# Four edits around the mixture-of-experts stages of a two-block float32 network: score banks by head, up rows beside the ring, last tile's logits token-major, a gathering quarter inside the first gate

## The reference

```python
aff = softmax(h @ router)                       # 16 experts
gate, idx = top_k(swapaxes(aff, 1, 2), cap)     # every expert takes 32 tokens of each stream
xs = h[bidx, idx]
hid = silu(einsum('becd,edf->becf', xs, w_gate)) * einsum('becd,edf->becf', xs, w_up)
y = einsum('becf,efd->becd', hid, w_down) * gate[..., None]
return zeros_like(h).at[bidx, idx].add(y)
```

## Time and profile before

| | us |
|---|---|
| median of 3 runs (2447.03 to 2451.07) | 2450.55 |
| profiled execution, its own time | 2450.56 |
| its span, first to last instruction | 2448.4 |
| TensorE busy | 2302.1 |
| VectorE busy | 1230.4 |
| ScalarE busy | 402.9 |
| DMA: 658.43 MB, mean rate over the span | 269 GB/s |
| mean granted clock of TensorE | 0.994 |

### The profile page before, as it was taken

One profiled execution on the slowest core, in us unless ns is written; L12 is line 12 of the kernel. 1 busy time (PEld: TensorE's weight loads), 2 busy tenths in 40 slices (PEclk: granted clock), 3 DMA queues, 4 the chain that ended last, 5 costly groups with the idle time before them and its releaser, 6 DMA issues. The chain is left out here.

```text
span 2448.4 us, 31994 instructions
## 1 busy us (share of the span) xinstructions
PE 2302.1 (94%) x13618; PEld 1477.8 (60%) x13618; DVE 1230.4 (50%) x2141; ACT 402.9 (16%) x885; POOL 38.6 (2%) x69
## 2 busy tenths in 40 slices
PE   8999999999999999999999998898899999988887
PEld 8898799499987994746644433333488543222222
DVE  7987777689877876935633221212265631111111
ACT  1221100002211010215621100000232420000001
POOL 0000000000000010000000000000000000000000
PEclk9999999999999999999999999999999999999999
DMA  9655765476557664512228999999941299999997
GB/s 325 241 166 197 229 211 213 158 258 241 172 190 247 201 227 143 212 45 52 93 110 349 421 429 427 427 427 428 404 150 35 94 359 416 428 427 428 428 428 321
DMA packets 170128, 658.43 MB, mean 269 GB/s; under 512 B 8551, under 2 KB 56163, under 8 KB 145411
## 3 DMA queue, kind: packets, MB, share of 16 engines
q1 hardware_dynamic: 164304, 639.66, 67.0%
q0 software_dynamic: 5312, 16.57, 2.2%
q10 hardware_dynamic: 370, 0.15, 0.0%
HBM read 655.12 MB, written 1.23 MB: 268 GB/s over the span
## 5 line engine op out<-in xcount | busy, mean ns | idle before, releaser
L881 PE MATMUL psum<-ring,arena 128*64 128x512 f32 (+2 forms) x2036 | 437.6, 583 | 56.1 <-DMA ring<-in_moe_w_up 35.3
L881 PEld LDWEIGHTS psum<-ring,arena 128*64 128x64 f32 (+1 forms) x2036 | 128.3, 123 | 338.8 <-issue 301.1
L912 PE MATMUL psum<-ring,lnp 128*32 128x512 f32 (+1 forms) x988 | 223.4, 598 | 35.2 <-DMA ring<-in_moe_w_down 34.9
L1806 DVE TENSOR_TENSOR lnp<-arena,psum 128x512 f32<-128x512 f32 (+2 forms) x32 | 33.8, 1056 | 411.5 <-PE psum L881 403.4
L1816 DVE TENSOR_TENSOR arena<-psum,spare 32x512 f32<-32x512 f32 x96 | 65.8, 686 | 230.3 <-PE psum L912 229.4
L2496 PE MATMUL psum<-ht,ring 128*128 128x128 f32 x1472 | 174.7, 277 | 2.5 <-DMA ring<-in_w_in 2.5
L912 PEld LDWEIGHTS psum<-ring,lnp 128*32 128x32 f32 (+1 forms) x988 | 63.7, 123 | 187.4 <-issue 149.7
L2496 PEld LDWEIGHTS psum<-ht,ring 128*128 128x128 f32 x1472 | 169.6, 193 | 6.3 <-issue 6.3
L580 PE MATMUL psum<-ring,ht 128*128 128x512 f32 x320 | 140.0, 594 | 0.0
L1227 ACT ACTIVATE lnp<-psum 128x512 f32<-128x512 f32 (+1 forms) x32 | 15.7, 490 | 625.6 <-PE psum L842 620.0
L2930 DVE SCALAR_TENSOR_TENSOR spare<-ring,arena,spare 128x512 f32<-128x512 f32 x168 | 113.8, 745 | 0.0
(11 more groups left out here) (555 smaller groups left out, 3278.1 us busy)
## 6 DMA issues: line engine op xcount, KB each, us to landing
ring<-in_moe_w_gate SPq DMA_DIRECT2D x62, 2048.0 KB
ring<-in_moe_w_up SPq DMA_DIRECT2D x61, 2048.0 KB
ring<-in_moe_w_down SPq DMA_DIRECT2D x57, 2048.0 KB
ring<-in_w_in SPq DMA_DIRECT2D x51, 1024.0 KB, 9.0
ring<-in_ada_w SPq DMA_DIRECT2D x48, 1024.0 KB
ring<-in_w_ffn_gate SPq DMA_DIRECT2D x22, 1024.0 KB
ring<-in_w_ffn_up SPq DMA_DIRECT2D x22, 1024.0 KB
ring<-in_w_ffn_down SPq DMA_DIRECT2D x20, 1024.0 KB
```

The lines of the kernel that those rows point to most:

```text
L881: last = mm(bank[w * j:w * j + w, 0:cols], (x_last if layer else x_four)[:, k, e % 4, :], row[:, cols * j:cols * j + cols], start=k == 0, ...
L912: last = mm(bank[w * j:w * j + w, :], hidT[:, e % 2, a:a + w], row[:, HALF * j:HALF * j + HALF], start=f == 0, stop=f == KT - 1)
L1806: TTo(view(hid_e[r, e % 2, 0:4 * c], 4, c), view(sil_e[r, e % 2, 0:4 * c], c, 4).rearrange("p c i -> p i c"), view(bank[r, 0:4 * c], c, 4) ...
```

## The change

1. **Score banks.** In layer 0's mixer the planner's order of a pair becomes s(h,0), s(h,1), s(h,2), s(h+1,0), s(h+1,1), s(h+1,2), so these lie in banks 4, 5, 6, 7, 0, 1. TensorE's own order stays as it was; only the counting of its events follows the new order.
2. **Up rows.** In layer 0 all four rows of u1's first panel lie outside the ring (the fourth in two pieces of the buffer `lnp`, loaded after the gate broadcast `gbc`); that panel leaves the ring, so each later panel stands one slot earlier. In layer 1 y0's row returns to the ring. y0 and its like wait for event `lg` instead of `lgT`.
3. **First panel in halves.** The first ring panel after g0's first half, in both layers, is loaded as two rows after two of g0's four rows, and two rows after all four.
4. **Logits.** All tiles but the last are routed as before, and copied and turned while the last tile is projected. The last tile's logits are formed token-major, straight into the bank that VectorE reads: the 128 x 128 turned tokens are stationary, the 32 router columns are moving.
5. **Gather.** In layer 0 the fourth quarter (latent high) is gathered between rows 3 and 4 of g0.
6. `block_r`, the indices of experts 4 to 15, is written with one instruction for each stream.

```diff
-        steps += [("wo", 0, t)] + [R] * (t == last) + [("wo", 1, t)] + [R] * (t == last)
-    return steps + [("rT", last, 0), ("rT", last, 1), ("lgT",)]
+        steps += [("wo", 0, t)] + [R, ("lgT",)] * (t == last) + [("wo", 1, t)] + [R] * (t == last)
+    return steps + [("rT", last, 0), ("rT", last, 1)]
...
-            mix0 += [("s", h + n, j) for j in range(3) for n in range(2)]
+            mix0 += [("s", h + n, j) for n in range(2) for j in range(3)]
...
+def gather_key(layer, g, s, m):
+
+    if (layer, g, s, m) == (0, 0, LAT, 1):
+        return "exp0", ("x", 0, s, m)
+    return (f"exp{layer}", ("x", g, s, m)) if g else (f"moe{layer}", ("x", s, m))
+
+
+def aside(layer, kind, e):
+
+    return (layer, kind, e) == (0, "u", 1)
...
-            first = BankPlan.TICK if besides(layer, kind, e) else EV
-            order += turned * own + [first] + turned * (not own) + [(kind, e)]
+            first = BankPlan.TICK if besides(layer, kind, e) or aside(layer, kind, e) else EV
+            order += turned * own + [BankPlan.TICK] * ((kind, e) == ("g", 0)) + [first] + turned * (not own)
+            order += [("x", 0, LAT, 1)] * ((layer, kind, e) == (0, "g", 0)) + [(kind, e)]
...
-                    sp.wait_ge(pe_done, banks.full(f"mix{layer}", ("lgT",)))
+                    sp.wait_ge(pe_done, banks.full(f"moe{layer}", ("lg",)))
...
+                    if layer == 0:
+                        up_rows = rows_of("u", 1)[0]
+                        sp.dma_start(view(arena[:, 2048:4096], 2, D), up_rows[:, 0:2, :]).then_inc(side_rows_in, 16)
+                        sp.dma_start(S["spare"][:, D:2 * D], up_rows[:, 2, :]).then_inc(side_rows_in, 16)
+                        sp.wait_ge(pe_done, banks.full("moe0", ("gbc",)))
+                        for j in range(2):
+                            sp.dma_start(side_rows[3][j], up_rows[:, 3, HALF * j:HALF * j + HALF]).then_inc(side_rows_in, 16)
...
+                    if aside(layer, kind, e) and h == 0:
+                        continue
                     first, _, _ = banks.release[n[0] - RING]
-                    sp.wait_ge(pe_done, first)
+                    early = n[0] - RING == banks.stage_panels[f"exp{layer}"][0]
+                    sp.wait_ge(pe_done, first - early)
...
+                    elif early:
+                        a = 2
+                        sp.dma_start(dst[:, 0:2, :], rows[h][:, 0:2, :]).then_inc(panel_in[slot], 16)
+                        sp.wait_ge(pe_done, first)
...
-                    mm(both[n], k[n][:, P * j:P * j + P], q[n], start=True, stop=True).then_inc(pe_done, 1)
+                    last = mm(both[n], k[n][:, P * j:P * j + P], q[n], start=True, stop=True)
+                    if n == 0:
+                        last.then_inc(pe_done, 1)
...
-                        last.then_inc(pe_done, 1)
+                        last.then_inc(pe_done, 3 if n else 1)
...
+            rows = 32 * len(tiles) - 32
+            wait_emptied(pe, stage, ("lgT",))
+            logits = open_bank(pe, f"moe{layer}", ("lg",))
+            nc.tensor.transpose(logits[:, 0:rows], logit_T[0:rows, :], ident[0:rows, 0:rows])
             pe.wait_ge(Q["half_ready"], base + len(tiles))
             raw_T(last_tile, 0)
             pe.wait_ge(Q["streams_ready"], base + len(tiles))
             raw_T(last_tile, 1)
-            route(logits, tiles[-1:], range(4))
-            route(logits, tiles[-1:], range(4, KT)).then_inc(pe_done, 1)
+            for k in range(KT):
+                if k % 4 == 0:
+                    wait_emptied(pe, stage, ("rT", last_tile, k // 4))
+                last = mm(logits[:, rows:rows + 32], rT[:, k, P * last_tile:P * last_tile + P],
+                          rtc[:, layer + last_tile // 2, k, :], start=k == 0, stop=k == KT - 1)
+            last.then_inc(pe_done, 1)
...
-            gather(stage, 0, ("x",))
+            gather(stage, 0, ("x",), quarters[:3])
...
+                    if k == 4 and (layer, kind, e) == (0, "g", 0):
+                        gather(stage, 0, ("x", 0), quarters[3:])
...
-                    if k % 4 == 3:
+                    if k % 4 == 3 or (kind, e, k) == ("g", 0, 1):
                         last.then_inc(pe_done, 1)
```

More of the change, by code:

```diff
@@ L744, in raw_T, with route @@
                 transposes(stage, ("rT", t, m), [tokens[t][:, P * k:P * k + P] for k in range(4 * m, 4 * m + 4)])
-            def route(bank, some, ks):
-                for k in ks:
+            def route(bank, some):
+                for k in range(KT):
                     if k % 4 == 0:
@@ L803, in moe, with gather, gathered @@
                block_0[:, src[0]:, :].rearrange("p a b -> p (a b)"), start=True, stop=True).then_inc(pe_done, 1)
[L805 to L817, removed]
+            def gather(stage, g, key, some):
+                for s, m in some:
+                    bank = open_bank(pe, stage, key + (s, m))
+                    for k in range(4):
+                        c0 = HALF * m + P * k
+                        for t in range(TT):
+                            last = mm(bank[:, P * k:P * k + P], xh[:, 2 * s + t, c0:c0 + P], pick[:, s, t, g, :],
+                                      start=t == 0, stop=t == 1)
+                    last.then_inc(pe_done, 1)
+            quarters = [(s, m) for m in range(2) for s in src]
+            def gathered(g, m):
                 for s in src:
-                    wait_emptied(pe, stage, key + (s, m))
+                    wait_emptied(pe, *gather_key(layer, g, s, m))
             keep_busy(stage, ("x", src[0], 0), 1, SEQ)
@@ L851, in up @@
                         turned(between)
[L852 to L858, removed]
+                    if k == 4 and (layer, kind, e) == (0, "g", 0):
+                        gather(stage, 0, ("x", 0), quarters[3:])
+                    beside_rows = aside(layer, kind, e) and k < 4
+                    if k % 4 == 0:
+                        if beside_rows:
+                            pe.wait_ge(side_rows_in, 64)
+                        elif besides(layer, kind, e):
                             if kind == "g":
@@ L865, in up @@
                         if kind == "g" and e % 4 == 0:
[L866 to L871, removed]
+                            gathered(e // 4, k // 4)
+                    if beside_rows:
+                        row = None
                     elif not besides(layer, kind, e):
@@ L957, in moe @@
                             wait_emptied(pe, stage, ("idx", s))
-                    gather(stage, e, ("x", e))
+                    gather(stage, e, ("x", e), quarters)
                 else:
@@ L1056, in tiles_in @@
                 if last:
+                    rows = 32 * len(tiles) - 32
+                    bank, freed = full_bank(act, stage, ("lgT",))
+                    A(logit_T[0:rows, :], bank[0:rows, 0:P], ACT.Copy).then_inc(freed, 1)
                     take(stage, ("rT", t, 0), rT[:, 0:4, P * t:P * t + P])
@@ L1201, in moe @@
             tiles_in(layer, tiles)
-            rows = 32 * len(tiles)
-            bank, freed = full_bank(act, f"mix{layer}", ("lgT",))
-            A(logit_T[0:rows, :], bank[0:rows, 0:P], ACT.Copy).then_inc(freed, 1)
             act.wait_ge(Q["shift_ready"], layer + 1)
@@ L1209, in moe, with gathered @@
             gates_out(stage, src, gb_moe)
-            def gathered(stage, key):
+            def gathered(g):
                 for m, s in enumerate(src):
-                    bank, freed = full_bank(act, stage, key + (s, 0))
+                    bank, freed = full_bank(act, *gather_key(layer, g, s, 0))
                     for k in range(4):
@@ L1219, in gathered @@
                     ins.then_inc(freed, 1)
-            gathered(stage, ("x",))
+            gathered(0)
             stage = f"exp{layer}"
@@ L1751, in moe, with gathered @@
             ins.then_inc(freed, 1)
-            blocks(block_r, 4, EXPERTS)
-            def gathered(stage, key):
+            for m, s in enumerate(src):
+                ins = TTo(block_r[s].rearrange("p (e n) -> p e n", n=SLOTS),
+                          own[:, m, 4:EXPERTS].unsqueeze(2).to_broadcast([64, EXPERTS - 4, SLOTS]),
+                          top_idxf.unsqueeze(1).to_broadcast([64, EXPERTS - 4, SLOTS]), ALU.mult)
+            ins.then_inc(Q["block_ready"], 1)
+            def gathered(g):
                 for m, s in enumerate(src):
-                    bank, freed = full_bank(dve, stage, key + (s, 1))
+                    bank, freed = full_bank(dve, *gather_key(layer, g, s, 1))
                     for k in range(4):
@@ L1852, in moe @@
                 elif kind == "x":
-                    gathered(stage, ("x", e))
+                    gathered(e)
                 elif kind == "c":
```

37 lines of the change are left out of this document (12 added, 25 removed).

## The result

The changed kernel takes 2453.2 us (median of 22 runs, 2450.01 to 2458.11) where the kernel before takes 2449.58 beside it (22 runs): ratio 1.0013, interval 1.0007 to 1.0019, that is 3.2 us more, between 1.7 and 4.7. The forecast was 1.9 more, "the same" by its bound of 0.2%. By that bound the two are the same, though the interval leaves out zero: the change costs a little. The profiled execution took 2453.91. Its span is 2451.8, 3.4 longer than that of the kernel before.

A forecast was written before the change was run, and what follows sets the result against it. TensorE's end of g2's first half was taken to set each layer's end. Layer 0's path (+1.8 - 0.7 + 1.6 = +2.7) gave stream +2.5, layer 1 -0.6: together +1.9, 2452.5 us, range 2446.5 to 2456.0.

The forecast's parts named there:

- The bound: Expert stages: each layer's end is set by when TensorE ends g2's first half; earlier loads only lengthen the gap before it.
- tie: Layer 0 at g3's panel: weights and TensorE arrive together, stream start 1349.9 by the g2 rule against 1350.1 by bytes.
- Up rows and halves: 0: Loads after g0: fewer ring bytes and an earlier first panel gain 0, since g3's panel still waits for g2's first half.
- Rival A: The restart of the weight stream sets the end: -6.2 together, 2444.4 us, faster; chance 0.10.
- Gather: +1.6, bounds to +1.8: Layer 0's g0: TensorE waits for the fourth quarter to be emptied, +1.6 on its path, bounds +1.4 to +1.8.
- Logits: -0.7 and -0.6: Behind the last route: copy and turning leave the path, -0.7 in layer 0, -0.6 in layer 1, bounds -0.4 to -0.8 each.
- Rival B: New idle inside g0 or the score pairs brings the clock to 0.50, costing 3.4: 2455.9 us, slower; chance 0.08.
- the route itself: Last route with eight 128-column passes behind its wait: change 0, bounds -0.5 to +0.7.
- Score banks: +1.8, gain 0: Layer 0's mixer: pairs 2, 4 and 6 each wait +0.6, +1.8 together; gain 0, at most 2.8.
- The argument from the clock row: Head 0's outputs: at half rate TensorE reaches the third bank near 1121, after VectorE emptied it near 1120.8; no removable wait.
- Rival C: Head 0's outputs had been held by their bank: -2.8 on top, 2449.7 us; chance 0.20.
- The sum: Layer 0's TensorE path +2.7, stream +2.5; layer 1 -0.6; together +1.9, 2452.5 us; chance as summed 0.62.

The follow-up runs named there:

- kernel 6: Changed kernel without the moved quarter and with the old score-bank order, plus y0 moved behind u2 in layer 0: 2446.05 us, ratio 0.9985.
- kernel 7: As kernel 6, with g2 also moved ahead of u1 in layer 1: 2444.34 us, ratio 0.9977.
- kernel 4: Kernel before with only the up rows outside the ring, the first panel in halves and the `block_r` edit: 2449.52 us, ratio 1.0004.
- kernel 5: Changed kernel without the moved gather quarter and with the old score-bank order, leaving logits and loads: 2450.79 us, ratio 1.0001.
- kernel 9: Changed kernel with filler matmuls in four waits (head 0's outputs, layer 1's turned heads, last tile's halves in both layers): 2448.14 us, ratio 0.9993.
- kernel 1: Kernel before with only the score-bank order changed, first head's three banks first: 2451.36 us, ratio 1.0006.
- kernel 2: Kernel before with only the fourth gathered quarter moved between the halves of g0 in layer 0: 2452.03 us, ratio 1.0011.
- kernel 3: Kernel before with only the last tile's token-major logits, in both layers: 2449.77 us, ratio 1.0000.
- kernel 8: As kernel 3, with two filler matmuls in layer 1's wait between the last tile's halves: 2449.26 us, ratio 0.9998.
- kernel 12: Kernel before with fillers only before head 0's outputs and behind layer 1's first turned heads: 2446.31 us, ratio 0.9984.

## Why the prediction was right, and where not

*The whole.* The forecast absolute time, 2452.5, is 0.7 from the measured 2453.2, but part of that is luck: the kernel before ran at 2449.58 beside it and not at 2450.55. The difference is the fair comparison: 3.2 was measured (1.7 to 4.7) and 1.9 forecast, near the lower end of that interval.

*The bound.* Right. Both reorderings (kernels 6 and 7) shorten their layer, by 2.9 and 1.8 in the traces. Layer 1's gap in front of g3 was to grow by about 2 and grew by some 1.2 (349 GB/s from 2033 to 2041 in the kernel before, 285 from 2036 to 2044 after). The "tie" in layer 0 was not exact. From g3's issue to SyncE's first load of layer 1's mixer it takes 376.3 to 377.0 in the four traces with a gap in front (the changed kernel, kernels 4, 5, 9), and 376.9 to 378.4 in the six where bytes still queued (the kernel before and kernels 1, 2, 3, 8, 12), means 376.7 and 377.7. So before the change the weights were on average one us behind what the rule says, and an edit that brings the first issue forward gets about that much back; the spread inside each set, 0.7 and 1.5, stays unexplained.

*Up rows and halves: 0.* Right within what the times tell (-1.2 to +3.2); by the traces nearer to -1 in layer 0, by the means above. Rival A is out.

*Gather: +1.6, bounds to +1.8.* Mechanism and place right, size short: 1.97. The wait is 1.55, as forecast. What the sum left out is that two runs of matmuls cut into four take 0.4 longer (5.62 + 2.05 for 7.41, twice 3.65 for 7.09).

*Logits: -0.7 and -0.6.* Layer 0 exact (6.50 for 7.21). In layer 1 the clock undid it: +0.6 in the changed kernel (1986.23 to 1993.58, 7.35 for 6.76), +1.4 in kernel 3, and at the full clock with one filler matmul -0.7 (kernel 9: 1981.37 to 1987.40). This is the step of the prediction that failed: the sum took the clock behind layer 1's last route as unchanged. Rival B had the mechanism but not its place. It looked for a low clock behind the new waits of 0.86 and 1.6 and not behind a route that had become light. The condition it gave, "if a stall of 1.6 is enough", was wrong too: TensorE idled 1.55 in g0 without a fall and 0.75 before this route with one.
On the route itself the bound held where the clock was full. It takes 2.03 with sixteen 128-column loads, eight of them behind the wait, and 1.93 with the 32-column loads of the kernel before. The Trainium skill's rule on weight loads (TensorE: Matmul & The Clock Gate, section on LDWEIGHTS), read as if nothing overlapped, gives an estimate of 0.6 more for the eight and 1.3 for the sixteen; this trace has 0.1. Sixteen loads of 0.19 each are 3.0 us of loading, and they lie within those 2.03, so they overlap.

*Score banks: +1.8, gain 0.* The cost is exact in two traces. The gain is 0 only while the clock is low. The argument from the clock row was right for that trace (at half rate TensorE comes after the bank is free), and kernel 6 beside the changed kernel confirms it. But "I see no wait there to remove" was read as a property of the kernel. At the full clock there is a wait, and it is worth 0.9. Rival C's 2.8 is out: the other 1.9 of it was the clock. Head 0's outputs were to be 7.4 long again; they were 6.3, because the low stretch happened to be 3.4 and not 6.8 long.

*The sum.* From the second projection of layer 0's mixer the path grew by 1.8 - 0.7 + 2.0 = 3.1, and with the 0.2 by which the traces stood apart there this is the 3.27 of g3's issue; 2.7 was forecast. That the two traces stood only 0.2 apart is luck: the changed kernel's was 1.3 behind at the start of head 0's outputs, and its shorter low stretch gave 1.1 back. SyncE's loads behind layer 1's mixer (1946.18 for 1943.55) were 2.6 later, where 2.5 was forecast for the layer. In layer 1 another 0.7 was added where 0.6 was to be saved, which gives the 3.34 at layer 1's g3 issue and the 3.4 at the end. Of the 1.5 by which the profiled difference exceeds the forecast, 1.3 is the logits of layer 1.

## What to carry to other kernels

Find the event after which nothing in a stage can move any more, and ask of each edit whether it moves that event. An earlier start in front of it mostly lengthens a gap, and work that frees no buffer belongs behind it. Before removing or lightening TensorE work next to a wait, ask what keeps the clock up: here, in layer 1, a route with a quarter of the moving columns behind 0.75 of idle time cost more than it saved, and one filler matmul in the wait gave it back. A low clock also hides waits, so a "no gain" that was read at 1.2 GHz has to be read again at 2.4. The fastest kernel here (11) keeps the logits and the loads, drops the moved quarter, has the banks by head in the first pair alone, reorders y0 and g2, and fills four waits: 2439.2 against 2450.3. Kernel 10, with the old order of banks, is as fast within the noise.

## What the runs showed of the hardware

After idle times of 3.5 and 4.2 the granted clock was at 1.2 GHz in 18 of 20 chances, for 3.4 or 6.8 us each; with filler that left 0.7 to 1.1 of idle it stayed at 2.4 in 8 of 8. The same code at the same wait gave low stretches of either length or none from run to run (head 0: 6.8 before, 3.4 after the change, none in kernels 4 and 5), and that alone moved head 0's outputs by some 2 between kernels with the same code there (5.5 in kernel 4, 7.5 in kernel 3). The Trainium skill (TensorE: Matmul & The Clock Gate, the section on its second failure mode) has the clock oscillate where TensorE idles only briefly but often between groups of matmuls. Layer 1's last route agrees in one point, that a short idle time can be enough: it is 0.75, and the clock fell in 5 of 5. It does not show the "often": one such wait stands before this route. An idle time of 1.07 before the old, denser route brought no fall in 10 chances (both layers of five traces), and one of 1.55 between dense matmuls none in 3. Why layer 0's last route, with the same new form behind 0.98 of idle time, fell in 3 of 6 only, is open.
